# Products with the condition turned round, convolution taps and shifted columns shared out anew, in a two-block transformer kernel

## The reference

```python
mod = silu(c) @ ada_w + ada_b                      # 1024 x 6144: six vectors of 1024
sh_mix, sc_mix, gt_mix, sh_ffn, sc_ffn, gt_ffn = split(mod, 6)
u = rmsnorm(x, norm_mix_g) * (1 + sc_mix) + sh_mix
p = u @ w_in                                       # 512 x 1024 @ 1024 x 2816
y_conv = conformer_conv(p[:, :1024], ...)          # a * sigmoid(b), causal depthwise convolution of 31 taps
y_rwkv = rwkv7_mix(p[:, 1024:], ...)               # token shift, low-rank products, a recurrence over tokens
x = x + gt_mix * (concat([y_conv, y_rwkv]) @ w_out)
...
def token_shift(p, mu):
    prev = pad(p, one row in front)[:-1]
    return p + mu * (prev - p)                     # = (1 - mu) * p + mu * prev
```

## Time and profile before

| | |
|---|---|
| median of 3 runs | 3484.43 us (3481.3 to 3489.3) |
| the profiled execution | 3488.55 us, of which the span of the instructions 3486.7 |
| PE busy | 2830.9 us (81%) |
| DVE, ACT, POOL busy | 1972.3 (57%), 1422.5 (41%), 1657.8 (48%) |
| mean granted TensorE clock | 0.904 |

### The profile page before, as it was taken

One profiled execution on the slowest core, in us unless ns is written; L12 is line 12 of the kernel. 1 busy time (PEld: TensorE's weight loads), 2 busy tenths in 40 slices (PEclk: granted clock), 3 DMA queues, 4 the chain that ended last, 5 costly groups with the idle time before them and its releaser, 6 DMA issues.

```text
span 3486.7 us, 43689 instructions
## 1 busy us (share of the span) xinstructions
PE 2830.9 (81%) x15610; PEld 2214.2 (64%) x15610; DVE 1972.3 (57%) x4255; ACT 1422.5 (41%) x3175; POOL 1657.8 (48%) x1014
## 2 busy tenths in 40 slices
PE   7966897796778887779688878679887988988898
PEld 6855896682333332266377766457666978987897
DVE  2666444356777777676665557676555453244422
ACT  2212222223333433356654445764443444343442
POOL 2712221254444533455166665356772516752674
PEclk9977998898999999988789998899997989989999
DMA  6310001227999999779679988888894314532453
GB/s 246 114 49 13 1 1 49 86 71 307 422 421 421 421 420 417 318 309 354 230 281 346 353 335 297 315 326 340 331 352 148 127 35 150 168 114 63 131 167 103
DMA packets 140520, 797.50 MB, mean 229 GB/s; under 512 B 15505, under 2 KB 18705, under 8 KB 67601
## 3 DMA queue, kind: packets, MB, share of 16 engines
q0 software_dynamic: 73728, 536.90, 38.3%
q1 hardware_dynamic: 65856, 253.36, 21.5%
q10 hardware_dynamic: 720, 4.46, 0.3%
HBM read 788.10 MB, written 6.55 MB: 228 GB/s over the span
## 4 chain that ended last, share of the span: by engine, by line
PE 44%; DMA 17%; DVE 12%; POOL 12%; issue 8%; ACT 6%; ACTq 0%; DVEq 0%; SPq 0%; POOLq 0%
DMA raw<-in_peer_uv,un 8%; PE ps L328 7%; PE ps L2395 7%; PE ps L1665 6%; POOL wls L298 6%; PE ps L808 6%; PE ps L1863 5%; DMA un<-in_peer_uv,un 3%; POOL wlw L298 3%; DMA w<-in_peer_uv,un 3%; PE ps L2373 2%; DVE scratch L1764 2%; PE ps L421 2%; POOL raw L1646 1%; DVE ps L1746 1%
## 5 line engine op out<-in xcount | busy, mean ns | idle before, releaser
L298 POOL TENSOR_TENSOR wls<-raws,whs 128x1024 fp32r<-128x1024 f32 (+1 forms) x256 | 605.9, 2381 | 399.2 <-ACT whs L292 397.9
L1665 PE MATMUL ps<-raw,un 128*128 128x512 f32 x760 | 409.4, 654 | 134.3 <-ACT un L1721 131.0
L1646 POOL DMA_INDIRECT raw<-in_peer_uv,un x276 | 281.6, 1020 | 383.9 <-DVE ps L1746 178.7
L1714 ACT ACTIVATE un<-un 128x1 f32<-128x1 f32 x512 | 103.6, 202 | 694.7 <-DVE scratch L1764 677.2
L292 ACT CAST whs<-raws 128x1024 fp32r<-128x1024 f32 (+1 forms) x256 | 260.8, 1036 | 194.8 <-PE ps L2395 85.7
L298 POOL TENSOR_TENSOR wlw<-raws,whw 128x1024 fp32r<-128x1024 f32 x112 | 265.6, 2387 | 107.2 <-ACT whw L292 106.9
L1863 PE MATMUL ps<-ts,whs 128*128 128x256 f32 x1424 | 303.0, 314 | 15.7 <-DVE ts L1932 9.6
L1665 PEld LDWEIGHTS ps<-raw,un 128*128 128x128 f32 x760 | 137.8, 204 | 279.9 <-ACT un L1721 199.8
L2395 PE MATMUL ps<-ts,whs 128*128 128x256 f32 x1216 | 258.6, 308 | 32.9 <-POOL wlw L298 27.1
L1863 PEld LDWEIGHTS ps<-ts,whs 128*128 128x128 f32 x1424 | 244.0, 207 | 45.4 <-issue 33.7
L1665 PE MATMUL ps<-w,un 128*128 128x512 f32 x384 | 201.8, 669 | 77.1 <-ACT un L1721 77.1
(11 more groups left out here) (421 smaller groups left out, 7171.4 us busy)
## 6 DMA issues: line engine op xcount, KB each, us to landing
raws<-in_w_up SPq DMA_DIRECT2D x128, 512.0 KB, 4.0
raws<-in_w_down SPq DMA_DIRECT2D x128, 512.0 KB, 4.3
raws<-in_w_qk SPq DMA_DIRECT2D x32, 512.0 KB, 7.4
scratch<-in_ada_w SPq DMA_DIRECT2D x13, 1024.0 KB, 15.1
raw<-in_w_in SPq DMA_DIRECT2D x11, 1024.0 KB, 5.1
raw<-in_ada_w SPq DMA_DIRECT2D x11, 1024.0 KB, 4.9
raw<-in_peer_w_q SPq DMA_DIRECT2D x8, 1024.0 KB, 7.2
raws<-in_w_v SPq DMA_DIRECT2D x16, 512.0 KB, 4.4
```

What stands on the lines that cost most here:

```text
L298: e.tensor_tensor(self.wl[h][:, 0:width], self.raw[slot][:, 0:width], self.wh[h][:, 0:width].bitcast(F32), ALU.subtract).then_inc(*self.ti ...
L1646: e.indirect_dma_start(self.rows[r], None, self.d["peer_uv"], index).then_inc(*self.tick(f"row{r}", n, 16))
L1665: ins = e.matmul(self.ps[:, b + half, :], self.diag[n % 4], self.rows[self.row_of(n)][:, 1024 + 512 * half:1536 + 512 * half], start=k == ...
```

## The change

There are three edits.

First, the products with the condition are turned round. `pe_mod_row` has a column of `silu(c)` as weights and a 128x256 piece of `ada_w` moving: eight products for a chunk, whose result is a row of 256 on one partition. VectorE copies the row out of PSUM (`dve_mod_row`), and `pe_mod` turns each piece of 128 into a column, by a product against a 1x1 one. Chunk 7 is no longer a chunk of TensorE; VectorE runs `mod_product` on it. The chunks of `prep` move: 13 and 14 behind the tiles w and a, 15 and 16 behind the head rows, 17 and 18 before the bonus, 19 at the end.

```diff
+    def pe_mod_row(self, e, tile, S, parts, freed):
...
+            for k in range(8):
+                ins = e.matmul(self.ps[0:1, b, 256 * n:256 * n + 256], self.small[:, k:k + 1], w[:, k, :], start=k == 0,
+                               stop=k == 7)
+        ins.then_inc(*self.tick(S, tile))
+
+    def dve_mod_row(self, e, tile, S, pe, row):
+        e.wait_ge(*self.at(pe, tile))
+        n = row.shape[1]
+        e.tensor_copy(row, self.bk(tile)[0:1, 0:n]).then_inc(*self.tick(S, tile))
...
+            for j in range(row.shape[1] // 128):
+                ins = e.matmul(self.ps[:, b, at:at + 1], row[:, 128 * j:128 * j + 128], self.C("ones")[0:1, 0:1],
+                               start=True, stop=True)
+                at += 1
...
-        self.dve_mod(e, "mod0", S, P_, 0, 16)
+        e.wait_ge(*self.at("ada7", 7))
+        self.mod_product(e, self.half(8), S, ("made", 7))
+        self.dve_mod_row(e, "row3", S, P_, rows[1][1])
+        self.dve_mod_row(e, "row6", S, P_, rows[2][1])
+        self.dve_mod(e, "mod0", S, P_, [(2 * n, 2) for n in (1, 4, 7, 0, 2, 3, 5, 6)])
```

Second, ScalarE makes the first half of the shift, and VectorE does seven taps a tile in place of nine:

```diff
+                elif j >= 8:
+                    e.wait_ge(*self.at("mix_pe", ("w_in", j)))
...
+                    e.activation(self.shifted(j - 8), self.bk(("w_in", j)), ACT.Identity, bias=0.0,
+                                 scale=omu[:, j - 8:j - 7]).then_inc(*self.tick(S, ("shift", j - 8)))
             if n + 2 < len(WIN_ORDER):
                 self.act_hi(e, ("w_in", WIN_ORDER[n + 2]))
...
-                e.tensor_scalar(dst, ps, omu[:, i:i + 1], None, ALU.mult).then_inc(*self.tick(S))
-                e.wait_ge(*self.last(S))
+                e.wait_ge(*self.at(A_, ("shift", i)))
                 e.scalar_tensor_tensor(out=dst[:, 1:S_], in0=ps[:, 0:S_ - 1], scalar=self.V("rwkv_mu", i), in1=dst[:, 1:S_],
...
-                self.dve_conv(e, 9, S)
+                self.dve_conv(e, 7, S)
```

Third, the 22 taps that are left are done in `prep`, eleven on each side of the scans; ScalarE's copies of the convolution move behind g, and TensorE keeps to four banks until the head sums are done:

```diff
+        mod(13, 2)
+        self.banks = NBANK
+        for i in range(4):
+            self.freed[4 + i] = ((A_, ("conv", i)),)
         self.pe_head_rows(e, R, "kk", S, D_, lambda q: (D_, ("kk", q)))
-        mod("mod16", (16, 17))
+        row(15, 16)
         tmp = fmat(self.half(17))
         for q in range(4):
+            if q == 0:
+                mod(15, 2)
+                row(17, 18)
             tile(("bonus", q), self.C("bd"), tmp[:, q, :], [(D_, ("rk", q))], (D_, ("bonus", q)))
-        mod("mod18", (18, 19))
+        mod(17, 2)
+        row(19)
+        mod(19, 1)
...
+        self.dve_conv(e, 11, S)
         for q in range(4):
             e.wait_ge(*self.at(A_, ("w", q)))
             e.tensor_tensor_scan(cum[:, q, :], self.scanm, sg[:, q, :], 0.0, ALU.mult, ALU.add).then_inc(*self.tick(S))
-        self.dve_mod(e, "mod8", S, P_, 16, 10)
+        self.dve_conv(e, len(self.conv_todo), S)
+        self.dve_mod(e, "mod8", S, P_, [(16, 10)])
+        row = self.rtmp[0:1, :]
+        self.dve_mod_row(e, ("row", 13), S, P_, row)
```

More of the change, by code:

```diff
@@ L411, in pe_mod @@
             e.wait_ge(*self.at(*f))
-        for n, (w, whole, ready) in enumerate(parts):
+        for n, (w, ready) in enumerate(parts):
+            w = w.rearrange("p (k n) -> p k n", n=256)
+            for f in ready:
+                e.wait_ge(*self.at(*f))
+            for k in range(8):
[6 more added lines that the diff above has]
+        e.tensor_copy(row, self.bk(tile)[0:1, 0:n]).then_inc(*self.tick(S, tile))
+    def pe_mod(self, e, tile, S, parts, rows, freed):
+        b, before = self.bank(tile, freed)
+        for f in before:
+            e.wait_ge(*self.at(*f))
+        at = 0
+        for w, ready in parts:
             w = w.rearrange("p (k n) -> p k n", n=256)
@@ L480, in act_mix @@
                          scale=1.0).then_inc(*self.tick(S, ("uh", i)))
-        sig = fmat(self.half(10))
+        sig, omu = fmat(self.half(10)), self.small[:, 16:30]
         for n, c in enumerate(WIN_ORDER):
@@ L590, in pe_mix, with row @@
         e.wait_ge(*self.at("ld_const", 0))
[L591 to L604, removed]
+        places = (0, 1, 2, 3, 4, 5, 7, 8)
+        def row(tile, *chunks):
+            self.pe_mod_row(e, tile, S, [(self.half(places[n]), [("mix_act", "silu"), (f"ada{n}", n)]) for n in chunks],
+                            (D_, tile))
+        row("row0", 0, 2)
+        e.wait_ge(*self.at(D_, ("sq", 7)))
+        self.pe_sums(e, self.gel[0], "sums", S, (D_, "sums"))
+        row("row3", 3, 5)
+        self.pe_spread(e, "rstd", S, D_, (D_, ("y", 7)))
+        row("row6", 6)
+        parts = [(self.half(places[n]), [(made, ("made", n))]) for n, made in ((1, "mix_pool"), (4, "mix_pool"), (7, D_))]
+        self.pe_mod(e, "mod0", S, parts, [(r, [(D_, tile)]) for tile, r in self.mix_rows()], (D_, "mod0"))
         self.banks, self.nbank = 4, 0
@@ L621, in pe_prep, with row @@
         R = [self.half(17)[:, 0:512], self.half(17)[:, 512:1024]]
-        def mod(tile, chunks):
+        def row(*chunks):
             parts = []
@@ L644, in pe_prep @@
             tile(("a", q), self.w2a2[64:128, c], lo[64:128, 0, :], [("ld_a2", 0)], (A_, ("a", q)))
-        parts = [(self.half(i), False, [("mix_pool", ("made", 8 + n))]) for n, i in enumerate((1, 2, 3, 7, 5))]
-        self.pe_mod(e, "mod8", S, parts, (D_, "mod8"))
+        parts = [(self.half(i), [("mix_pool", ("made", 8 + n))]) for n, i in enumerate((1, 2, 3, 7, 5))]
+        self.pe_mod(e, "mod8", S, parts, [], (D_, "mod8"))
+        row(13, 14)
         for q in range(4):
@@ L683, in act_prep @@
             e.copy(g[:, q, :], self.bk(("g", q))).then_inc(*self.tick(S, ("g", q)))
+        for i in range(4):
+            e.wait_ge(*self.at(D_, ("conv", i, CW - 1)))
+            e.copy(conv[:, i, :], self.ps[:, 4 + i, :]).then_inc(*self.tick(S, ("conv", i)))
         stat = self.small[:, 204:236]
```

70 lines of the change are left out of this document (39 added, 31 removed).

## The result

| | before | after |
|---|---|---|
| median | 3485.90 us (4 runs) | 3438.73 us (4 runs) |
| the profiled execution, its span | 3488.55, 3486.7 | 3435.03, 3433.1 |
| normalised x begins | 67.32 | 54.26 |
| the projection's last tile is ready | 198.40 | 181.48 |
| norm's maximum | 259.99 | 211.49 |

The ratio is 0.9864, with a 95% interval of 0.9846 to 0.9881: 47 us less, inside the range and 13 us above the forecast. Up to the chunk stage the two profiles differ by 50.6 us, where 60.4 were forecast. The span from the start of the chunk stage to the end is 3179.9 us before and 3176.9 after; over the nine experiments it lies between 3173 and 3187, untouched as its code is. So a single run's time tells little under 10 us, and from here on I compare the start of the chunk stage, and the starts ahead of it.

A forecast was written before the change was run, and what follows sets the result against it. The prediction took the chain of waits in the 306.8 us before the chunk stage as what the change moves. From 3488.5 us, less 24.5 (prologue) and 35.9 (projection and preparation), it got 3428 and said 3426, range 3410 to 3462.

The forecast's parts named there:

- the likeliest case: Whole kernel: streaming through one weight column raises the clock and all parts gain, 3426 us; chance 0.60.
- The clock: TensorE's row products: streamed columns raise the clock, so a chunk takes 3.4 us after the first few us, against 6.95 before.
- The first rival: TensorE's rows: one weight column doesn't count for the clock, 3460 or 3456 us; chance 0.25 with its half way, 3447.
- Part 1: Prologue: normalised x starts at 42.8 us instead of 67.32, -24.5 us; -5 us at the low clock.
- Part 2: Projection: TensorE sets the pace at 5.44 us a column tile, ending at 194.5 instead of 198.4 us.
- Part 3: Preparation up to the chunk stage: end at 270.7 against 306.6, -35.9 us, of which 3.9 is the projection's.
- The second: Rival, projection and preparation: VectorE's taps stay on the path, some -20 instead of -36 us, 3443 us; chance 0.08.
- The third: Rival, TensorE's rows: the weight load isn't hidden under its own stream, so the change is slower, 3494 us; chance 0.04.

The follow-up runs named there:

- u1_prep: The changed kernel with the old products at the new places of the preparation and no copies of rows; chunk stage 1.3 us sooner than in the changed kernel.
- c2_pool_waits: The changed kernel with one wait added, so GpSimd begins the low parts of w_in only after VectorE has folded chunk 7; chunk stage at 249.87 us.
- c3_kf_late: The changed kernel with GpSimd's product Kf put off until VectorE is at products that read PSUM; 2.6 us less at the chunk stage.
- u2_shift_dve: The changed kernel with both halves of the shift on VectorE again, seven taps a tile; it cost 15.1 us at the chunk stage.
- u3_taps_in_mix: The changed kernel with nine taps a tile in the projection and none left for the preparation; chunk stage 5.9 us later.
- p2_only: The kernel before with ScalarE's half of the shift alone, nine taps a tile, old products and old order; chunk stage 14.0 us sooner.
- u1_prologue: The changed kernel with the old products and old order in the prologue alone, chunk 7 on TensorE; normalised x at 66.81 us, 12.6 us later.
- c1_row7: The changed kernel with chunk 7 made as a row on TensorE, without VectorE's product; normalised x at 46.20 us, ratio to the kernel before 0.9837.

## Why the prediction was right, and where it wasn't

The direction and the likeliest case held, and 47 us came of 60. By its steps:

- *The clock.* The rows reached the high clock, from 0.42 to 0.21 us a record after 5 us. The forecast had chunks 0 and 2 done at 25.0; their unbroken series ended at 25.2. That it is the streaming which counts, as the prediction took it, is not shown: no run takes apart what the clock answers to, and in u1_prep the old form had the high clock for 5 us. The first rival (3456 to 3460) is out: in the preparation too the pairs 15, 16 and 17, 18 took 7.07 us each, the price of the high clock. The prediction gains 5 us in the prologue even at the low clock; its walk has no wait for GpSimd's chunk 1, which took 4.4 us before, but it doesn't name this term.
- *Part 1, -24.5 forecast, -13.1 measured: the step that failed.* It is VectorE's walk, the product of 2.3 us and "additions of half, a quarter and an eighth of that, 4.4 in all: 36.2" (31.6 and 4.4 are 36.0, which changes nothing). The prices were taken from a row in which GpSimd idled, and laid beside GpSimd at work. VectorE was done at 47.87: product and additions took 14.6 us from 33.29 on, of which c2_pool_waits removes 8.4 by keeping GpSimd's two subtractions apart. It started at 33.3 and not at 31.6, behind the diagonals (5.81 us), for which the sum has no term. So the folding, which the forecast starts at 37.8, could go on only at 47.9, and the 24 of its 32 records behind this wait took 5.4 us at the low clock, where the sum had 3.6 for all 32. With the subtractions apart x began at 43.81, 1.0 from the forecast.

The Trainium skill (SBUF — State Buffer, "Who interferes with whom") has this rule: a VectorE instruction with two inputs from SBUF contends with a GpSimd instruction that reads SBUF, and the later of the two is shut out altogether. c2_pool_waits and c3_kf_late agree, with 11.19 against 2.82 us and 6.85 against 2.74, and so do the turns of whole instructions shown above; so do the taps, with one SBUF operand and one in PSUM, which take the same with GpSimd and without. It should have stood among the rivals. As an estimate from this case's rows, its price was 9 us of part 1 (11.19 less 2.82, and 3.35 less 2.29).

- *Part 2, -3.9 forecast, -3.9 measured.* A tile takes 5.44 us, as reckoned, TensorE's pace. But the sum took both edits for it, and one is enough: u2_shift_dve (seven taps, whole shift on VectorE, 6.1 us a tile) and u3_taps_in_mix (nine taps, ScalarE's half of the shift) have the same 127.2 us, and so has p2_only with 6.44 us a tile. At 7.43 us a tile, before, it was 131.1. That the four banks take up what VectorE falls behind is argued and not tested.
- *Part 3, -32 forecast beyond part 2, -33.7 measured.* The norm comes 30.0 us after the projection (33), `Bf` 46.2 (48.7), the chunk stage 74.8 (76.2). VectorE's taps and scans went as walked (the last tap 24.4 us after the projection, 24.8 forecast); the last g tiles and the head sums ran at the high clock, 1.98 and 3.63 us where the sum has 3.5 and 4.3. The sum was near and one of its reasons wrong: the prediction lets 13 us of this part hang on the rows' clock, and u1_prep, with the old products and no copies, loses none of them. What is left is the order (nothing of 20.6 us stands ahead of w and a any more), which no run isolated; some 16 us remain when shift (15), taps (6) and prologue (14) are taken from 50.6, if they add up.
- *Rivals.* The second (taps stay on the path) was half true: they do lie on it, but VectorE kept 5.44 us a tile and TensorE waited only 1.16 us for the addition behind them, so part 3 kept its gain. The third (load not hidden) is out: rows went at 0.21 and 0.42 us a record. The prediction's estimate that a load of one column costs a hundredth of one of 128 did not hold, though: it stands at 0.13 us (19.97, above) where those of 128 columns at the same clock have 0.33. It stayed hidden all the same.
- The other 3 us between 50.6 and the 47 of the medians are within the spread of the untouched rest.

## What to carry over

Before work goes to VectorE, look what GpSimd does at that moment: with two SBUF operands on each side one of them stood still for a whole instruction of the other, and the length in a row where the other idled doesn't hold; an operand in PSUM or a wait that keeps the two apart avoided it. One SBUF operand can be enough, as the diagonals show. Weights of one column with the matrix streaming are worth it where TensorE would be slow otherwise; their result must then be copied and folded, and that copy must not stand ahead of the critical engine's next step. Undo each part of a change alone: here the same edit brought 13 us in one stage and nothing in the other. And see what else the undoing takes along, such as the old order in u1_prologue.

## Not expected of the hardware

- The diagonals are multiplications with only one SBUF operand and a scalar for each partition. Four took 0.87 us alone and 5.81 beside GpSimd, also in c1_row7, where only chunk 4 lay beside them. Two of the four have all the loss (the changed kernel):

```profile
27.56 3.13 DVE L347 TENSOR_SCALAR scratch<-kept 128x128 f32<-128x128 f32 x1
30.81 2.36 DVE L347 TENSOR_SCALAR scratch<-kept 128x128 f32<-128x128 f32 x1
```

  The first ends at 30.7, just after GpSimd's product (27.01 to 30.61), and the third at 33.2, just after GpSimd's first addition (30.69 to 33.09); the other two take 0.27 us each. The Trainium skill (SBUF — State Buffer, "Who interferes with whom") counts this operation among those that can take the port pair shared with GpSimd; the trace agrees, and no run set out to test it.
- The product with 128 weight columns and one moving column doesn't always run slow: behind the head rows it began at the high clock and kept it for some microseconds (48 records in 5.00 us, then 30 in 6.00), and behind the bonus tiles it took 4.17 us for 32 records.
